# Spacing out the requests for x's pieces at the start of a hybrid encoder step

## The reference

```
h = x @ w_in                      # 2176 x 1024 times 1024 x 3584
u, v, z_a, q, k, v_b, z_b = split(h)       # 512 columns each
a = gelu(u) * (tril(w_sgu) @ layernorm(gelu(v)) + b_sgu)     # chunks of 128 frames
b = softmax(q k^T / 8 + relative bias) @ v_b  # own chunk of 64 frames and 8 before, 8 heads
y = concat(a * silu(z_a), b * silu(z_b))
out = layernorm(alpha * x + y @ w_out)
```

## Time and profile before

| | |
|---|---|
| median of three runs | 1063.88 us |
| the profiled execution | 1063.93 us, of it 1062.2 us span |
| TensorE busy | 1049.7 us (99%) |
| VectorE, ScalarE, GpSimd busy | 454.0, 360.0, 132.6 us (43%, 34%, 12%) |
| granted TensorE clock, mean | 0.998 of full speed |
| DMA, first three of 40 slices of 26.6 us | 338, 207, 186 GB/s |
| DMA, mean | 121 GB/s |

### The profile page before, as it was taken

One profiled execution on the slowest core, in us unless ns is written; L12 is line 12 of the kernel. 1 busy time (PEld: TensorE's weight loads), 2 busy tenths in 40 slices (PEclk: granted clock), 3 DMA queues, 4 the chain that ended last, 5 costly groups with the idle time before them and its releaser, 6 DMA issues.

```text
span 1062.2 us, 17679 instructions
## 1 busy us (share of the span) xinstructions
PE 1049.7 (99%) x7342; PEld 910.5 (86%) x7342; DVE 454.0 (43%) x952; ACT 360.0 (34%) x728; POOL 132.6 (12%) x144
## 2 busy tenths in 40 slices
PE   9999999999999999999999999999999999999997
PEld 7988888999999999999999888777888888888885
DVE  6535442202122211111123000587777777767665
ACT  6410001111111111111212112566666666666630
POOL 0111111020101000000000000013222222233201
PEclk9999999999999999999999999999999999999999
DMA  9561113222221233342331161794544444433222
GB/s 338 207 186 40 41 49 114 82 70 82 72 67 52 94 127 115 109 148 101 130 127 70 59 186 60 222 276 145 160 139 132 141 139 146 138 111 110 93 77 80
DMA packets 111999, 128.43 MB, mean 121 GB/s; under 512 B 7192, under 2 KB 85680, under 8 KB 111920
## 3 DMA queue, kind: packets, MB, share of 16 engines
q1 hardware_dynamic: 107456, 112.62, 32.9%
q10 hardware_dynamic: 4464, 14.68, 4.3%
HBM read 82.17 MB, written 48.26 MB: 123 GB/s over the span
## 4 chain that ended last, share of the span: by engine, by line
PE 95%; SPq 2%; DMA 1%; ACT 1%; DVE 1%; issue 0%; POOLq 0%; POOL 0%; DVEq 0%; ACTq 0%
PE s_ps L1260 35%; PE s_ps L1277 17%; PE out_ps L1468 15%; PE pt_ps L1260 8%; PE o_ps L1432 6%; PE s_ps L1361 5%; PE pt_ps L1403 3%; PE s_ps L1468 2%; PE s_ps L1390 1%; PE o_ps L1289 1%; DMA offset<-ln_b 1%; PE out_ps L1289 1%; DMA x_raw<-x_t 1%; SPq L539 0%; PE o_ps L1446 0%; SPq L651 0%
## 5 line engine op out<-in xcount | busy, mean ns | idle before, releaser
L1260 PE MATMUL s_ps<-xh,ring 128*128 128x384 f32 (+1 forms) x1152 | 327.7, 362 | 0.8 <-ACT st L829 0.8
L1260 PEld LDWEIGHTS s_ps<-xh,ring 128*128 128x128 f32 x1152 | 212.4, 188 | 23.9 <-issue 1.2
L1260 PE MATMUL s_ps<-xl,ring 128*128 128x384 f32 (+1 forms) x576 | 208.7, 362 | 0.0
L1277 PE MATMUL s_ps<-ring,xh 128*128 128x512 f32 x544 | 169.8, 393 | 0.0
L1277 PEld LDWEIGHTS s_ps<-ring,xh 128*128 128x128 f32 x544 | 100.5, 188 | 20.5 <-issue 0.3
L1260 PEld LDWEIGHTS s_ps<-xl,ring 128*128 128x128 f32 x576 | 108.1, 188 | 11.6
L868 ACT ACTIVATE prob<-prob,low 128x640 f32<-128x640 f32 (+3 forms) x128 | 97.5, 763 | 54.4 <-DVE low L1097 54.4
L1097 DVE CUSTOM_DVE_ANT_1 prob<-s_ps,bias 128x640 f32<-128x640 f32 (+1 forms) x112 | 85.7, 803 | 52.4 <-PE s_ps L1361 52.4
L1277 PE MATMUL s_ps<-ring,xl 128*128 128x512 f32 x272 | 106.0, 390 | 0.0
L1468 PE MATMUL out_ps<-wo_h,yh 128*128 128x512 f32 x248 | 99.9, 403 | 0.0
L1468 PE MATMUL out_ps<-wo_l,yh 128*128 128x512 f32 x248 | 96.8, 391 | 0.0
(11 more groups left out here) (150 smaller groups left out, 1261.9 us busy)
## 6 DMA issues: line engine op xcount, KB each, us to landing
raw<-w_all ACTq DMA_DIRECT2D x26, 512.0 KB, 3.6
r<-x SPq DMA_DIRECT2D x17, 512.0 KB, 3.6
q<-s_q SPq DMA_DIRECT2D x16, 512.0 KB, 4.4
k<-s_k SPq DMA_DIRECT2D x16, 512.0 KB, 5.9
y_out<-r SPq DMA_DIRECT2D x15, 512.0 KB, 2.7
x_raw<-x_t SPq DMA_DIRECT2D x12, 384.0 KB, 13.2
s_mix<-st SPq DMA_DIRECT2D x17, 256.0 KB, 2.3
v_all<-st SPq DMA_DIRECT2D x17, 256.0 KB, 2.1
```

Source lines behind the costliest of these rows:

```text
L1260: last = nc.tensor.matmul(bank[b][:, 0:width], w[:, kc, :], xx[:, kc, :], start=kc == 0 and a == 0, stop=kc == KC - 1 and a == 2)
L1277: last = nc.tensor.matmul(out, xx[:, kc, cols], ring[:, 0:GRP, side, kc, :], start=kc == 0 and a == 0, stop=kc == KC - 1 and a == 2)
```

## The change

In SP's first loop a wait is put ahead of seven of the 25 requests: m=4 to m=10 (`len(PIECES_OF[0])` is 9, so m is below 11). Each waits until piece m-3 has landed entirely. m=4 to m=8 are the last five pieces of chunk 0, m=9 and m=10 the first two of chunk 1. From m=11 on nothing is waited for. No transfer, size, destination or order of requests is altered, and no other engine's code.

```diff
--- before.py
+++ after.py
@@ -448,6 +448,8 @@
             for m in range(len(PIECES)):
                 c, held = piece(m)
                 t0, _ = CHUNKS[c]
+                if 4 <= m < len(PIECES_OF[0]) + 2:
+                    sp.wait_ge(x_loaded[m - 3], 16)
                 sp.dma_start(x_raw[c][held], x_t[:, held[1], t0 + held[2].start:t0 + held[2].stop]).then_inc(x_loaded[m], 16)
```

## The result

The changed kernel takes 1065.19 us (median of 17 runs, 1063.83 to 1066.85) against 1063.51 us of the kernel before in the same comparison (17 runs, 1062.42 to 1065.02): a ratio of 1.0015, 95% interval 1.0009 to 1.0021. That is 1.7 us slower, within the 0.2% called no change, inside the range, and not nothing. The two profiled executions, 1065.99 and 1063.93 us, differ by 2.1.

The account below looks back on a forecast made before the run. TensorE, busy 99% of the span, was taken as the bound, with only its 1.45 us start stall to win. Terms 0 + 0 + 0 on the profiled 1063.93 us gave 1063.9 us, range 1062.5 to 1065.3.

Parts of the forecast that it names:

- Where it can matter: Only TensorE's start, before 55 us, can pay or cost; quicker arrivals can win at most 1.45 us.
- Do the waits bind: On SP's queue: yes, requests move later, by 2.1 us (m=4) to 5.8 us (m=9).
- m=2 and m=3, value zero: Their requests keep places and times, so m=2 lands at 8.0 us as before; gain zero, at most 1.45 us.
- rival 1: At TensorE's stall before m=2: a shorter queue lands m=2 sooner, gain 0.3 to 1.4 us, 1062.9 us; chance 0.23.
- Rival 1's price: The gain from an earlier m=2, taken as 1.0 us, with some products perhaps at the clock's 1.2 GHz level.
- x, the time of a request in a short queue: For 256 KB among m=4 to m=10: taken as 3.04 us, middle 3.84, highest 6.3.
- m=10 to m=12 follow at 1.35 each: In chunk 1: these pieces land at the pace they are consumed, so their margin is m=9's, 0.2 us.
- Rival 2: Ahead of chunk 1: the short queue starves, m=9 lands late if 256 KB takes over 3.3 us; 1065.0 to 1069.9; chance 0.17.
- SP's later work: After m=10: a full queue again ends x's requests at 25.96 us; chunk 2 has 4.1 us margin; cost zero.

Follow-up runs that it names:

- e5: The changed kernel with waits only for m=6 to m=10, each on the piece five before; 1064.52 us, ratio 1.0001 to the kernel before.
- e2: The changed kernel with only the waits for m=9 and m=10 kept; 1065.80 us, ratio 1.0010 to the kernel before.
- e11: The kernel before, without waits, with 11 constant products ahead of x instead of 8; 1064.05 us.

## Why the prediction was right, and where it was not

The median lies in the range, 0.1 us under its upper end, and "within 0.2%" had 0.91. That it lies inside is in part luck: this end was worked out from 256 KB requests of 4.0 us, the delay came about in another way. The forecast itself, nothing beyond some tenths, was wrong by 1.3 us (1065.19 against 1063.9), and by 1.7 against the runs beside it. Step by step:

- **Where it can matter.** Right: the difference arises before 30 us, 2.6 us of it, and the rest of the kernel gives back half a microsecond.
- **Do the waits bind.** Right: the requests left 2.7 us (m=4, at 5.33) to 6.6 us (m=10, at 13.37) later than before; forecast for m=10 was 12.7, and for m=9 12.0 where it was 12.35.
- **m=2 and m=3, value zero.** Wrong; rival 1 happened too. In the eight profiles with a wait on m=4, m=2 landed at 6.5 to 7.3 us; in the five with no wait before m=9, at 7.5 to 8.8; in e5, whose first wait is on m=6, at 7.3. It brought nothing here, since chunk 1 had to wait all the same. The rule of the Trainium skill that I weighed against rival 1 ("DMA: Bandwidth & Descriptors", Queues, rings and completion order) does not forbid this: m=2's descriptors may be taken in order and its slowest engine still be held up by the requests behind. By what, no run shows.
- **Rival 1's price.** Mis-sized in the profile of after by the clock: I had "some products perhaps at the lower level"; it was all six of m=2, 2.44 us for 1.49, so m=3 started no sooner. Late landings in chunk 1 hid this too.
- **x, the time of a request in a short queue.** I took 3.04 for 256 KB. m=7 and m=8 took 2.8 and 2.9: right. m=4 to m=6, beside the weights, took 4.8 to 5.2: too small, and without effect there.
- **"m=10 to m=12 follow at 1.35 each".** This is the step that failed. m=9 landed at 16.45, within tenths of what chunk 1 could bear (15.93, and half a microsecond more as TensorE was late). m=10 followed 3.1 us behind it, not 1.35. I had priced the short queue as a delay of each request at the full 390 GB/s, and never asked what the engines had left to move; they ran dry (121 GB/s from 11 to 12 us), and afterwards the rate stayed low, 268 and 320 GB/s from 12 to 20 us, up to some 18 us, five after the last wait. Rival 2 had the place and the sign, and its threshold was on the wrong piece.
- **SP's later work.** SP ended x's requests at 29.5 us instead of 25.96, since the full queue came back later: my 25.96 was wrong. Chunk 2 had 4.1 us of margin and shows no wait. Cost zero, as said.

## What to carry to other kernels

Waiting for a landing before asking for the next piece costs more than the waits. A piece is seen to land some time after most of its bytes have moved, so count what the engines have left to move, not the pieces that have not landed. Here, with three pieces in the queue, they ran dry, moved a third less from 8.7 to 18.4 us, and took five microseconds after the last wait to recover; with five pieces, and waits that ended at 9.7 us, they lost almost nothing. If an early piece must come sooner, hold back only the requests directly behind it and let the queue fill again before the next tight place (here three waits measured 0.5 us below their base, too little to be sure of, where seven measured 1.1 above theirs). And count what a short wait of TensorE does to its clock, not only its length: in e2's profile chunk 0's products after a wait of 2.01 us took 1.6 us more than in the kernel before, and with three more products on constants the upper group of runs was gone.

Then look which piece sets the time. A gain or a loss ahead of a piece that is late anyway shows in no total.

## What was not expected of the hardware

- A wait of 2.01 us took TensorE's clock from the upper to the lower level, and the products behind it ran at 0.43 instead of 0.23 us (512 columns) up to 12.3 us. A wait of 2.31 us in e11's profile did not (mean clock 0.999). So such a wait may or may not cost clock.
- The first rise of the clock was as uneven: in the trace of before the products after 8.70 ran at the upper level, with the changed kernel those up to 10.5 us still at the lower, after 0.61 us without work at 4.89.
- The stretch table printed a granted clock of 1.00 in both those starts. The length of a product by its columns shows the level there, the column does not.
- After the engines have run dry, a full queue does not bring the rate back at once. In the changed kernel 277 GB/s were moved from 15 to 18 us with 2.1 MB waiting at 15 us; in e2, whose queue of old requests only shrinks from 6 to 11.7 us, 404 GB/s from 9 to 11 us with 1.0 MB waiting at 9 us and 0.56 at 10. At 11.5 us it has 0.04 MB left, and moves 57 GB/s from 12 to 13 us. After that its rate is uneven up to 18 us (391 GB/s from 14 to 15, 133 from 16 to 17), with 1.8 MB and more waiting. So it is not the depth of the queue by itself; why the rate is lower for some microseconds after such a gap, no run shows. Every kernel is slower still at its start (169 to 247 GB/s from 3 to 5 us). e2's stretches:

```profile
9.00:11.00 2.00, 2.00 (x6) 1.59 (x5) 2.00 (x4) 1.21 (x4) 0.00 (x0) 0.50 1.05 404
12.00:13.00 1.00, 1.00 (x5) 0.86 (x4) 1.00 (x3) 1.00 (x3) 0.00 (x0) 0.84 0.29 57
```
